# Fourteen of a layer's sixteen modulation chunks: from TensorE products to VectorE dot products on turned weights

## The reference, cut to what matters

```python
silu_c = jax.nn.silu(c)
silu_cc = jax.nn.silu(c_ctx)
for layer in range(DEPTH_2):                       # 2 layers
    mod_x = silu_c @ ada_w[layer] + ada_b[layer]   # (1024) @ (1024, 6144)
    mod_c = silu_cc @ ada_w[layer] + ada_b[layer]
    sh1, sc1, g1, sh2, sc2, g2 = [m[:, None, :] for m in jnp.split(mod_x, 6, axis=-1)]
    ...
    x = x + g1 * (mx @ w_out[layer])
    hx = modulate_2(rmsnorm(x, norm2_g[layer]), sh2, sc2)
    x = x + g2 * squared_relu_mlp(hx, w_mlp1[layer], w_mlp2[layer])
    # the context likewise, in layer 0 only
```

## Time and profile before

| what | value |
|---|---|
| median of 3 runs | 2018.05 us (2015.6 to 2018.36) |
| profiled execution, its own time | 2015.12 us |
| its span | 2013.3 us, mean granted TensorE clock 0.987 |
| TensorE busy | 1929.2 us, 96% of the span |
| VectorE, ScalarE, GpSimd busy | 754.5, 625.2, 392.5 us |
| layer 0's MLP, turns 1 to 7 and the down half of turn 0 | about 1239.8 to 1591 us of the span |

### The profile page before, as it was taken

How to read it: one execution, slowest core, us unless ns; L and a number is a source line. 1 busy time by engine, 2 the same in 40 slices (tenths; PEclk the granted TensorE clock), 3 DMA queues, 4 the chain that set the end, 5 groups by cost and what they waited for, 6 DMA issues and landing times.

```text
span 2013.3 us, 27741 instructions
## 1 busy us (share of the span) xinstructions
PE 1929.2 (96%) x11650; PEld 1396.9 (69%) x11650; DVE 754.5 (37%) x1241; ACT 625.2 (31%) x939; POOL 392.5 (19%) x205
## 2 busy tenths in 40 slices
PE   5999999999999999998999899999999999888998
PEld 2777786954444444446887657777777778678998
DVE  1625255632222222225343844222223535564333
ACT  2523113232222222213112534222333511545454
POOL 2000000110000000004002232333333210424664
PEclk9999999989999999998999999999999999999999
DMA  9469817559999999981323004444444223414451
GB/s 359 161 244 363 294 54 298 198 231 414 427 420 424 423 423 426 421 349 51 113 84 126 34 32 146 147 153 171 157 146 146 85 94 116 170 43 163 172 184 47
DMA packets 120215, 428.41 MB, mean 213 GB/s; under 512 B 5690, under 2 KB 23141, under 8 KB 107456
## 3 DMA queue, kind: packets, MB, share of 16 engines
q1 hardware_dynamic: 118016, 416.56, 53.7%
q0 software_dynamic: 2112, 10.57, 1.5%
HBM read 426.07 MB, written 1.05 MB: 212 GB/s over the span
## 4 chain that ended last, share of the span: by engine, by line
PE 64%; PEld 18%; issue 7%; DVE 4%; ACT 3%; POOL 2%; DMA 1%; PEldq 0%; DVEq 0%; POOLq 0%; SPq 0%; ACTq 0%
PE bank L532 62%; PEld bank L532 18%; PE bank L547 2%; DMA ring<-in_ada_w 1%; DVE H L1930 1%; DVE H_low L1937 0%; POOL arena L1845 0%; POOL arena L1844 0%; PEldq L511 0%; DVE arena L2450 0%; POOL arena L1849 0%; POOL arena_r L1885 0%; POOL arena L1847 0%; POOL arena L1850 0%; POOL ring_low L1871 0%
## 5 line engine op out<-in xcount | busy, mean ns | idle before, releaser
L532 PE MATMUL bank<-arena_r 128*128 128x512 f32 (+1 forms) x2304 | 634.3, 345 | 13.6 <-ACT arena_r L1351 5.4
L532 PE MATMUL bank<-arena_r,ring_low 128*128 128x512 f32 (+2 forms) x1920 | 597.2, 343 | 5.4 <-DVE H_low L1937 5.3
L532 PEld LDWEIGHTS bank<-arena_r 128*128 128x128 f32 x2304 | 404.3, 190 | 106.6 <-issue 48.4
L532 PEld LDWEIGHTS bank<-arena_r,ring_low 128*128 128x128 f32 (+1 forms) x1920 | 353.5, 189 | 51.4 <-issue 6.1
L532 PE MATMUL bank<-arena 128*128 128x64 bf16 (+8 forms) x2588 | 304.0, 282 | 26.8 <-DMA arena<-in_hy_filt_w 11.5
L532 PE MATMUL bank<-ring,arena 128*64 128x512 f32 x1024 | 278.2, 595 | 1.1 <-ACT arena L1531 0.7
L532 PEld LDWEIGHTS bank<-arena 128*128 128x128 bf16 (+4 forms) x2588 | 187.1, 131 | 129.6 <-issue 94.7
L532 PE MATMUL bank<-H_low,arena_r 128*128 128x512 f32 (+1 forms) x672 | 216.3, 339 | 0.0
L2508 DVE SCALAR_TENSOR_TENSOR X<-bank,mod,X 128x256 f32<-128x256 f32 x216 | 94.6, 479 | 316.9 <-PE bank L532 316.7
L1871 POOL TENSOR_TENSOR ring_low<-ring,arena_r 128x2048 fp32r<-128x2048 f32 x32 | 146.9, 4613 | 137.7 <-ACT arena_r L1721 70.1
L1365 ACT ACTIVATE arena<-bank 128x512 f32<-128x512 f32 (+2 forms) x106 | 51.2, 496 | 373.2 <-PE bank L532 373.0
(11 more groups left out here) (297 smaller groups left out, 1940.3 us busy)
## 6 DMA issues: line engine op xcount, KB each, us to landing
ring<-in_moe_w_gate SPq DMA_DIRECT2D x32, 2048.0 KB, 13.9
ring<-in_w_mlp SPq DMA_DIRECT2D x32, 2048.0 KB, 8.7
ring<-in_w_in SPq DMA_DIRECT2D x26, 2048.0 KB, 8.1
ring<-in_ada_w SPq DMA_DIRECT2D x24, 2048.0 KB, 11.9
ring<-in_moe_w_up SPq DMA_DIRECT2D x17, 2048.0 KB, 9.5
H<-in_moe_w_down SPq DMA_DIRECT2D x16, 2048.0 KB, 16.3
arena<-in_moe_w_up SPq DMA_DIRECT2D x15, 2048.0 KB, 9.6
ring<-in_moe_w_down SPq DMA_DIRECT2D x15, 2048.0 KB, 16.5
```

The lines of the kernel that those rows point to most:

```text
L532: ins = nc.tensor.matmul(o, l, r, start=start, stop=stop, skip_group_check=True)
```

## The change

Turn 0 keeps its two modulation chunks on TensorE (now turned into columns in turn 0 itself, where the kernel before gathers four chunks and turns them in the odd turn). For turns 1 to 7 the modulation weights come from a transposed copy in memory, `ada_t_2`, 384 rows of 1024 at a time, so that a partition holds three output features' whole weight rows. `dots` takes each such row against the silu of `c` and of `c_ctx` (`CSIL`, the vectors copied to all partitions by a new 1 MB load from GpSimd's queue and passed through one ScalarE activation in turn 0): one VectorE instruction of 1024 elements each, multiply with accumulated sum into a column of `mod`. That is 3 blocks x 2 vectors x 2 chunks = 12 instructions in a turn. Four blocks (8 instructions) stand ahead of the low part of w2, two blocks (4 instructions) behind it. Each block waits on `dots` for the one before (the product's scratch `CPROD` is used again). TensorE waits for `dots` to reach 6j behind the hidden tiles and then gives back w1 and both modulation chunks together. The bias is added in one instruction after the last turn. Two semaphores are merged with others (`sw_zero` into `selected`, and a count of `b2_in` moves by one load).

```diff
 # SP, per half h of pair i in layer 0
 for a in range(2):
-    load(n, cols(T["ada_w_2"][1], (i * 4 + h * 2 + a) * ADA_COLS, ADA_COLS), as_cols(n, ADA_COLS), i * per)
+    q = i * 4 + h * 2 + a
+    if isinstance(i, int) and h == 0:
+        load(n, cols(T["ada_w_2"][1], q * ADA_COLS, ADA_COLS), as_cols(n, ADA_COLS), i * per)
+    else:
+        load(n, rows(T["ada_t_2"], q * ADA_COLS, ADA_COLS), as_turned(n), i * per)
     n += 1
 # TensorE
-                ada(n + 1 + a, 7, 7, a, 4, ADA_COLS, release=False)
+                ada(n + 1 + a, 7, 7, a, 2, ADA_COLS, release=False)
...
-        chunk_used(3 if early else 1)
-        n += 1
-        if early:
-            n += 2
-        elif l == 0:
-            for a in range(2):
-                ada(n, 7 + i, 7, 2 * u + a, 4, ADA_COLS, turns)
-                n += 1
+        if l == 0 and not early:
+            pe.wait_ge(S("dots"), 6 * j)
+        chunk_used(1 if l else 3)
+        n += 1 if l else 3
         pe.wait_ge(S("w_split"), 9 + 8 * l + j + 1)
...
-            if (l, u, nt) == (0, 1, 3):
-                ada_turn(7 + i, 7, 0, 4, ADA_COLS)
+            if (l, j, nt) == (0, 0, 3):
+                ada_turn(7, 7, 0, 2, ADA_COLS)
 # ScalarE, after a turn's squares
-        if (l, u) == (0, 1):
-            ada_rows(7 + i, 7, 0, ADA_COLS)
+        if l == 0 and isinstance(i, int) and u == 0:
+            ada_rows(7, 7, 0, ADA_COLS)
+            act.wait_ge(S("b2_in"), 16 * 5)
+            A_(CSIL, CSIL, ACT.Silu).then_inc(S("silu_c"), 1)
 # GpSimd, ahead of its turns
+if l == 0:
+    bring(CSIL, T["c_all_2"].rearrange("p (a d) -> p a d", a=2), "b2_in")
 # VectorE
+        dotted = l == 0 and not (isinstance(i, int) and (i, u) == (0, 0))
+        if dotted:
+            dve.wait_ge(S("silu_c"), 2)
+            dots(i, u, range(4))
         dve.wait_ge(S("w_high"), 24 * l + (i * 2 + u) * 3 + 3)
         n = mlp_chunks(l, u, 1, i)[0]
         V.tensor_tensor(low(n), slot(n), W2h.bitcast(F32), ALU.subtract).then_inc(S("w_split"), 1)
+        if dotted:
+            dots(i, u, range(4, 6))
         for t in range(KT):
             dve.wait_ge(S("mlp_mm"), 64 * l + (i * 2 + u) * 8 + t + 1)
             add(t, ps[MLP_BANK[t % 4]], 40).then_inc(S("mlp_bank_free"), 1)
-            if (l, u, t) == (0, 1, 4):
-                take_chunk(2, 7 + i, 7, i * 12, 4, ADA_COLS)
+            if l == 0 and not dotted and t == 4:
+                take_chunk(2, 7, 7, 0, 2, ADA_COLS)
...
+def dots(i, u, blocks):
+    n0, turns = MLP0 + 4 * u + 1, i * 32
+    for q in blocks:
+        n = n0 + q // 3
+        if q % 3 == 0:
+            dve.wait_ge(full[n % RING], arrived(n) + turns)
+        if q or not (isinstance(i, int) and (i, u) == (0, 1)):
+            dve.wait_ge(S("dots"), i * 12 + u * 6 + q - 6)
+        for c in range(2):
+            d = V.scalar_tensor_tensor(CPROD[:, c, :], as_turned(n)[:, q % 3, :], 1.0, CSIL[:, c, :], ALU.mult, ALU.mult,
+                                       accum_out=mod[:, 2, bass.ds(i * 12 + u * 6 + q, 1), c])
+        d.then_inc(S("dots"), 1)
...
+        lo = VOFF["ada_b2"][0] + 48
+        link(V.tensor_tensor(mod[:, 2, 6:48, :], mod[:, 2, 6:48, :], bc(vecs[:, lo + 6:lo + 48].unsqueeze(2), [P, 42, 2]), ALU.add))
         gains(2)
```

More of the change, by code:

```diff
@@ L252, in as_rows, with as_turned @@
             return slot(n).rearrange("p (k n) -> p k n", k=4)
+        def as_turned(n):
+            return slot(n)[:, 0:3 * D].rearrange("p (b d) -> p b d", b=3)
         E5 = 8328 + 3 * 4096
@@ L344, in _, with mlp_loads @@
                     load(first + 16 + j, cols(T["w_out_2"][l], j * 512, 512), as_cols(first + 16 + j))
-                with sp.Fori(0, 4) as i:
+                def mlp_loads(i):
                     n = mlp
@@ L357, in _ @@
                         n += 1
+                if l == 0:
+                    mlp_loads(0)
+                with sp.Fori(1 - l, 4) as i:
+                    mlp_loads(i)
             for a in range(4):
@@ L492, in build @@
         MLP_BANK = (4, 5, 2, 3)
+        CSIL, CPROD = A3(12288, 2, D), A3(22944, 2, D)
         W1h_cols, W2h_rows = W1h.rearrange("p (k n) -> p k n", k=KT), W2h.rearrange("p (k n) -> p k n", k=4)
@@ L873, in _ @@
                        "logits" if (tb, k) == (1, 7) else None)
-            pe.wait_ge(S("sw_zero"), 1)
+            pe.wait_ge(S("selected"), 1)
             pe.wait_ge(S("h_rest"), 4)
@@ L880, in _ @@
                 stat(2, k, L, CSQ)
-            pe.wait_ge(S("selected"), 1)
+            pe.wait_ge(S("selected"), 2)
             mm(ps[5][:, 0:NX], SLT, SELX[:, 0, :])
@@ L1053, in _ @@
                         flush()
-                        pe.wait_ge(S("b2_in"), 16 * (4 + l))
+                        pe.wait_ge(S("b2_in"), 16 * (4 + 2 * l))
                         pe.wait_ge(S("tile_free"), tiles[0] - 4)
@@ L1852, in _ @@
                 pool.wait_ge(S("lgam"), l + 1)
-                pool.wait_ge(S("b2_in"), 16 * (4 + l))
+                pool.wait_ge(S("b2_in"), 16 * (4 + 2 * l))
                 head_args(0)
@@ L2166, in _ @@
             norm(1, 0, 1, (0,), False)
-            V.memset(SW, 0.0).then_inc(S("sw_zero"), 1)
+            V.memset(SW, 0.0).then_inc(S("selected"), 1)
             V.memset(RKM[:, :, NX:NX + 4], -1.0)
@@ L2230, in _ @@
             dve.wait_ge(S("ranks"), 1)
-            dve.wait_ge(S("selected"), 1)
+            dve.wait_ge(S("selected"), 2)
             link(V.scalar_tensor_tensor(RKM[:, :, 0:NX], ps[5][:, 0:2 * NX].rearrange("p (a b) -> p a b", a=2), 1.0, SELX, ALU.add, ALU.mult))
@@ L2377, in _ @@
                 dve.wait_ge(S("lgam"), l + 1)
-                dve.wait_ge(S("b2_in"), 16 * (4 + l))
+                dve.wait_ge(S("b2_in"), 16 * (4 + 2 * l))
                 for k in range(4):
@@ L2547, in mlp_pair @@
                                     i_.then_inc(full[(L1 + 1) % RING], 16)
-                with dve.Fori(0, 3) as i:
+                def dots(i, u, blocks):
[10 more added lines that the diff above has]
+                        d.then_inc(S("dots"), 1)
+                if l == 0:
+                    mlp_pair(0)
+                with dve.Fori(1 - l, 3) as i:
                     mlp_pair(i)
@@ L2552, in _ @@
                 if l == 0:
-                    dve.wait_ge(S("ada_out"), 2 + 11)
+                    dve.wait_ge(S("ada_out"), 2 + 8)
+                    dve.wait_ge(S("dots"), 42)
+                    lo = VOFF["ada_b2"][0] + 48
+                    link(V.tensor_tensor(mod[:, 2, 6:48, :], mod[:, 2, 6:48, :], bc(vecs[:, lo + 6:lo + 48].unsqueeze(2), [P, 42, 2]), ALU.add))
                     gains(2)
@@ L2580, with spread @@
         arrays[name] = I[name]
+    def spread(v):
+        return np.broadcast_to(v.reshape(1, -1), (P, v.size))
+    arrays["ada_t_2"] = np.ascontiguousarray(I["ada_w_2"][1].T)
+    arrays["c_all_2"] = np.ascontiguousarray(spread(np.concatenate([I["c_2"].reshape(-1), I["c_ctx_2"].reshape(-1)])))
     arrays["wr"] = np.concatenate([I["moe_router_g_w"][0], I["moe_router_e_w"][0].transpose(1, 0, 2).reshape(D, NX)], axis=1)
@@ L2591, in pad @@
         return a
-    def spread(v):
-        return np.broadcast_to(v.reshape(1, -1), (P, v.size))
     parts = {
```

## The result

The changed kernel takes 2024.65 us in the median of 8 runs (2023.61 to 2027.71); the kernel before took 2018.46 beside it (8 runs, 2015.6 to 2021.16). The ratio is 1.0036, with a 95% interval of 1.0023 to 1.0049: slower by 6.2 us, outside the 0.2% that I had called no change. The time forecast was 2016.4; the range (2002 to 2031) holds the measured one, but by luck: its upper end stands for rival 2, and the slowdown came from something that no term and no rival had. The profiled execution took 2024.97 us, 9.85 more than the one before (2015.12).

What follows compares the result with a forecast made beforehand. It took TensorE, busy 96% of the span, as the bound. Removed products replaced by the stall (+0.1 us over seven turns) and turning saved (-1.7) gave -1.6 from 2018.05: 2016.4 us, range 2002 to 2031.

Steps and rivals of the forecast that it cites:

- rival 2: VectorE's eight dots ahead of the low part: written-out sum above 0.15 us delays them; +12.9 us at 0.3; chance 0.18.
- What is removed, 2.81 us a turn and the turning: TensorE: 16 modulation products, 2.81 us in seven turns, and three turnings of 0.58, 1.7 us; 21.4 if all were gain.
- Eight dots ahead of the low part are hidden: VectorE's gap before w2's low part: eight dots end at 1273.26, 0.58 us before ScalarE's copy is done.
- The cost a of the written-out sum: Each VectorE dot: extra time on top of 1.22 us, taken as 0.08 us; hidden ahead of the low part until 0.15.
- rival 4: VectorE's dots: accumulating halves the fp32 rate, 1.1 us more for each; +80 us, 2098; chance 0.04.
- GpSimd gets in between every two dots and holds the port for 1.0 us: Behind w2's low part: three GpSimd tile parts each keep VectorE off the shared SBUF port for 1.0 us.
- rival 1: Dots behind the low part: GpSimd gets the port less often, or dots don't need it; -8.7 to -20.6 us; chance 0.22.
- rival 3: Dots behind the low part: port lost for GpSimd's full 1.29 us each time; +4.5 us, 2022.5; chance 0.04.
- The stall is 2.82 us: TensorE's wait on `dots` between the hidden and the down products, forecast at 2.82 us in a turn.
- The stall on `dots` takes the place of the products removed. Per turn +0.01: TensorE's down start in turn 1: 1286.50 against 1286.49 before; over seven turns 0.1 us.
- something not thought of: Anywhere in the kernel: a remainder outside the likeliest case and the four rivals, counted as slower; chance 0.02.
- What is moved costs nothing: w1 given back at the down start, 2.8 us later than before: next w1 load still hidden, with 1.2 us to spare.

Runs made afterwards that it cites:

- e6: Changed kernel, TensorE's wait on `dots` moved behind the third down tile, VectorE's last two blocks held until GpSimd's third tile part; 1997.25 us, ratio 0.9898.
- e4: Changed kernel with the four dots behind w2's low part reading 8 of their 1024 elements; 1994.48 us, ratio 0.9882 to the kernel before.
- e1: Changed kernel with sixteen unread products of 384 columns put into TensorE's gap ahead of the wait on `dots`; 2014.39 us, ratio 0.9991.
- e7: Changed kernel with w1 given back alone ahead of TensorE's wait on `dots`, the wait left in place; 2020.62 us, ratio 1.0021.
- e3: Changed kernel with five blocks of dots ahead of w2's low part and one behind, instead of four and two; 2006.07 us, ratio 0.9953.

## Why the prediction was wrong

The picture of the turn was right and one of its prices was missing. By its steps:

- **What is removed, 2.81 us a turn and the turning.** Right, and sized a little low: by the turns' lengths the products are 46.68 - 43.77 = 2.91 and a turning 47.37 - 46.68 = 0.69 instead of 0.58. In e6, where nothing stands in the way, about all of it comes back: 2017.92 - 1997.25 = 20.7 us (17.6 to 23.8 by the interval), where the forecast had 21.4 for everything.
- **Eight dots ahead of the low part are hidden.** Right, with 1.28 us to spare. The cost a of the written-out sum is a separate instruction of 0.08 us that lies beside the next dot (the next one starts with it): a = 0 for the time. Rival 2 (a above 0.15) is out, and rival 4 too: the instruction takes 1.22 us with the sum, as without. The halving that the Trainium skill's Vector Engine (DVE) Microarchitecture Reference states isn't seen here, with two fp32 sources in SBUF.
- **GpSimd gets in between every two dots and holds the port for 1.0 us.** Right in place and number: three of four dots are stretched, by 1.10, 1.08 and 0.97 us; e4 gives 1.09 and 0.99. Over the seven turns the third is stretched by less, 0.48 to 0.97, and the three together by 3.0 in the mean. That rules out rival 1 (fewer holds) and, by a little, rival 3: the full 1.29 us is not reached. The rule of the Trainium skill (SBUF — State Buffer, section "Who interferes with whom"), that the later side waits for the other's whole instruction, agrees in kind; by its words each wait would be 1.29 us, and the ones here are 0.2 us shorter and more.
- **The stall is 2.82 us.** Mis-sized by a little: 2.35 in turn 1, 2.45 in the mean. The dots behind the low part cost 0.26 less in turn 1 (a is 0), and the low part began 11.94 us behind the first hidden product instead of 12.14.
- **"The stall on `dots` takes the place of the products removed. Per turn +0.01".** This step failed. It set 2.8 us of standing still equal to 2.8 us of products, and took the down products behind it at the speed of the earlier trace rows. The products before had kept TensorE busy until the down start, in a stage with a clock of 1.00; with a stall in their place the clock goes to its lower level just behind it, for 3.4 us, and each turn loses 1.6 us: 7 x 1.6 = +11 us that no term of the sum held (the shorter stall gave 2.6 of them back). e1 shows it: the gap filled with products that nobody needs, the wait and the loads unchanged, and the slow stretches are gone from the profile. None of my four rivals had this mechanism; it is in the 0.02 for something not thought of. The Trainium skill (TensorE: Matmul & The Clock Gate, section "HAM oscillation — how this bites in real kernels") tells of a matmul loop with waits of 3 to 5 us that falls to the half clock after every one of them and pays for it again and again; these traces agree in kind, with seven falls behind seven waits, and theirs are shorter, 2.2 to 2.4 us.
- **What is moved costs nothing.** Right: w1's next part came in time, and e7 gives back w1 earlier without a shorter turn to speak of (47.79 against 47.93).

## What to carry to other kernels

Work on a busy TensorE is not only time, here it also kept the clock up. When work is taken off TensorE and comes back as a wait at one place, put a price on the products behind that wait too (here 3.4 us at half speed, 1.6 us lost, behind each wait of 2.0 to 2.5 us; nothing behind waits of 1.0 to 1.6), and read the granted clock behind the wait in the profile before you trust either figure elsewhere. Take the wait to where its condition is already true (here three output tiles later: some 26 us against the changed kernel from a moved wait), or leave some of the work there. And where VectorE and GpSimd both read SBUF at the same time, count 1 us for each 128x512 GpSimd part that gets in between, and put what has slack behind what TensorE waits for.

## What was unexpected of the hardware

- TensorE's clock went from 2.4 to 1.2 GHz after it had stood still for 2.2 to 2.4 us (in e7 2.0 to 2.5) in a stage in which it was otherwise busy all the time, in 7 of 7 turns of both profiles, for 3.4 us each time. The wide spacing began 0.6 to 1.5 us behind the down start, when work had already resumed. With 1.0 to 1.6 us of standing still at the same place (e3) it never did.
- The length of a wait doesn't decide it alone. Right behind layer 0's MLP TensorE waits 3.1 us for ScalarE in every profile. In the kernel before and in e1 to e4 the clock falls there, in the changed kernel, e6 and e7 it does not; and the kernel before keeps its clock behind a wait of 2.51 us some 16 us later. Waits and windows, the kernel before first, the changed one below it (engine columns as above). What decides between them no run here shows.

```profile
1597.48 0.36 PE L532 MATMUL bank<-arena_r 128*128 128x256 f32 x1 [3.14 <-ACT arena_r L1351]
1597.48:1602.48 5.00, 5.00 (x29) 5.00 (x30) 5.00 (x14) 2.98 (x8) 0.00 (x0) 0.66 0.00 0
1613.17 0.47 PE L532 MATMUL bank<-arena_r 128*128 128x512 f32 x1 [2.51 <-DVE ring_low L2354]
1613.17:1618.17 5.00, 5.00 (x22) 4.08 (x23) 0.00 (x0) 0.00 (x0) 0.00 (x0) 1.00 0.67 224
```

```profile
1604.39 0.36 PE L546 MATMUL bank<-arena_r 128*128 128x256 f32 x1 [3.13 <-ACT arena_r L1361]
1604.39:1609.39 5.00, 5.00 (x39) 4.80 (x40) 5.00 (x14) 2.98 (x8) 0.00 (x0) 1.00 0.00 0
```

- A VectorE instruction with a written-out sum shows as two rows, 1.22 and 0.08 us, and two such dots follow each other after 1.14 us (1263.76, 1264.90): the sum is free.
- In turns without any wait of TensorE, 84 dots of 1.2 us on VectorE did not slow TensorE's products at all: 192 of them take 43.77 us from down start to down start, 0.228 apiece (e6), as before without the modulation products (46.68 - 2.81 = 43.87).
